# Conditioning of a two-layer diffusion block folded vector by vector: layer 1's residual and second-norm vectors for the latent stream only

## The reference, cut to what matters

```
sh1, sc1, g1, sh2, sc2, g2 = split(c_act  @ w_mod[l] + b_mod[l])     # latent stream
mod_c                      = split(cc_act @ w_mod[l] + b_mod[l])     # context stream
h  = rms_norm(x, ln1_g) * (1 + sc1) + sh1;   proj = h @ w_in[l]
x  = x + g1 * merge(three branches of proj) @ w_o
h2 = rms_norm(x, ln2_g) * (1 + sc2) + sh2
x  = x + g2 * (silu(h2 @ w_ff1) * (h2 @ w_ff3)) @ w_ff2
```

## Time and profile before

| | us |
|---|---|
| median of three runs | 1314.69 (1313.2 to 1316.62) |
| the profiled execution | 1312.58 |
| its span | 1310.8 |
| TensorE busy | 1233.6 (94% of the span) |
| VectorE busy | 915.6 (70%) |
| ScalarE busy | 531.1 (41%) |
| mean granted TensorE clock | 0.981 of full speed |

### The profile page before, as it was taken

One profiled execution on the slowest core, in us unless ns is written; L12 is line 12 of the kernel. 1 busy time (PEld: TensorE's weight loads), 2 busy tenths in 40 slices (PEclk: granted clock), 3 DMA queues, 4 the chain that ended last, 5 costly groups with the idle time before them and its releaser, 6 DMA issues.

```text
span 1310.8 us, 19521 instructions
## 1 busy us (share of the span) xinstructions
PE 1233.6 (94%) x7212; PEld 1031.6 (79%) x7212; DVE 915.6 (70%) x1372; ACT 531.1 (41%) x876; POOL 53.5 (4%) x52
## 2 busy tenths in 40 slices
PE   4999999999997979999999999779999998999997
PEld 3777766677876868887888788468888888999997
DVE  4554777768777777764676677777788876666565
ACT  4432555522423344322322223245664555544444
POOL 2000000000000300000000000200000002000002
PEclk9999999999998989999999999889999999999999
DMA  8837322024466516644565554324433574666562
GB/s 281 250 98 238 96 56 65 33 77 117 116 190 193 157 52 195 191 148 147 155 180 156 165 161 125 101 80 124 114 107 97 152 202 129 192 178 192 174 175 69
DMA packets 281599, 187.63 MB, mean 143 GB/s; under 512 B 12795, under 2 KB 270129, under 8 KB 281521
## 3 DMA queue, kind: packets, MB, share of 16 engines
q1 hardware_dynamic: 281521, 186.57, 48.6%
HBM read 185.49 MB, written 1.05 MB: 142 GB/s over the span
## 4 chain that ended last, share of the span: by engine, by line
PE 83%; DVE 8%; issue 4%; ACT 3%; DMA 1%; ACTq 0%; DVEq 0%; SPq 0%; POOL 0%; POOLq 0%
PE bank L1633 20%; PE bank L1635 20%; PE bank L1634 20%; PE scores L1885 2%; PE bank L1668 2%; PE bank L1669 2%; PE bank L1676 2%; DVE Wlo L355 2%; PE bank L1868 2%; PE probsT L1894 2%; PE bank L1870 2%; PE bank L1869 2%; ACT Whi L344 1%; PE attended L1905 1%; DVE RSTD L1149 1%
## 5 line engine op out<-in xcount | busy, mean ns | idle before, releaser
L1633 PE MATMUL bank<-Hhi,Whi 128*128 128x512 f32 (+2 forms) x1216 | 413.7, 340 | 6.4 <-DVE Wlo L355 6.4
L1635 PE MATMUL bank<-Hhi,Wlo 128*128 128x512 f32 (+2 forms) x1216 | 409.6, 337 | 0.0
L1634 PE MATMUL bank<-Hlo,Whi 128*128 128x512 f32 (+2 forms) x1216 | 409.6, 337 | 0.0
L355 DVE TENSOR_TENSOR Wlo<-Wraw,Whi 128x1024 fp32r<-128x1024 f32 (+4 forms) x328 | 320.5, 991 | 112.5 <-ACT Whi L344 110.9
L344 ACT ACTIVATE Whi<-Wraw 128x1024 fp32r<-128x1024 f32 (+4 forms) x330 | 277.6, 862 | 152.3 <-PE bank L1635 94.7
L1633 PEld LDWEIGHTS bank<-Hhi,Whi 128*128 128x128 f32 (+1 forms) x1216 | 229.9, 189 | 37.7 <-DVE Wlo L355 7.0
L1634 PEld LDWEIGHTS bank<-Hlo,Whi 128*128 128x128 f32 (+1 forms) x1216 | 230.0, 189 | 25.8 <-issue 1.2
L1635 PEld LDWEIGHTS bank<-Hhi,Wlo 128*128 128x128 f32 (+1 forms) x1216 | 229.9, 189 | 25.1
L1633 PE MATMUL bank<-Uhi,Whi 128*128 128x512 f32 (+1 forms) x480 | 164.3, 342 | 0.7 <-DVE Ulo L1161 0.6
L1634 PE MATMUL bank<-Ulo,Whi 128*128 128x512 f32 (+1 forms) x480 | 162.7, 339 | 0.0
L1635 PE MATMUL bank<-Uhi,Wlo 128*128 128x512 f32 (+1 forms) x480 | 162.5, 339 | 0.0
(11 more groups left out here) (169 smaller groups left out, 1412.2 us busy)
## 6 DMA issues: line engine op xcount, KB each, us to landing
Wraw<-in_w_ff SPq DMA_DIRECT2D x120, 512.0 KB, 3.8
Wraw<-in_w_in SPq DMA_DIRECT2D x78, 512.0 KB, 3.8
ATT<-in_w_mod SPq DMA_DIRECT2D x56, 512.0 KB, 4.2
Wraw<-in_w_o SPq DMA_DIRECT2D x16, 512.0 KB, 4.7
ACC<-in_w_mod SPq DMA_DIRECT2D x12, 512.0 KB, 3.9
Wraw<-in_w_ff SPq DMA_DIRECT2D x16, 384.0 KB, 3.2
Wraw<-in_w_mla_o SPq DMA_DIRECT2D x8, 512.0 KB, 3.4
PR<-in_w_mod SPq DMA_DIRECT2D x8, 512.0 KB, 4.3
```

What stands on the lines that cost most here:

```text
L355: last = eng.tensor_tensor(lo, raw, hi.bitcast(F32), ALU.subtract)
L1633: pe.matmul(dst, sh, mh, start=j == 0, stop=False)
L1634: pe.matmul(dst, sh, ml, start=False, stop=False)
L1635: last = pe.matmul(dst, sl, mh, start=False, stop=j == k - 1)
```

## The change

Folds now go by vector, not by turns of two. In the branches only vector 4 of layer 0 is folded (8 transfers, both streams). Along the FFN come seven vectors of 8 transfers: vector 5 of layer 0 (both streams), vectors 0 and 1 of layer 1 (both), vectors 2 to 5 of layer 1 (latent stream only: one fold instruction instead of two, and half the matmuls of the sum). The sums over 256 columns stand behind FFN tiles 14, 24, 34, 42, 50, 58 and 66; the transposes (two instead of four) one tile behind each, and those of the last at the start of layer 1. VectorE adds each vector to MOD in the tile of its transposes; vector 5 of layer 0 is read from tile 16 on. ScalarE's part of layer 0's FFN is written out instead of looped. In the projection the last four transfers of vectors 2 and 3 are issued later: 12 and 13 behind the load of chunk 14, 14 and 15 behind that of chunk 15, before behind chunks 12, 13, 14 and 15.

```diff
-HALF_AFTER_LOOK = [10, 11, 17, 18, 19, 21, 22, 23, 26, 27, 30, 31, 32, 33, 34, 35]
-TURN_AFTER_LOOK = [b + j for b in (0, 24) for j in (2, 4, 5, 6, 8, 9, 10, 12, 13, 14, 16, 17, 18, 19, 20, 21)]
-TURN_AFTER_LOOK += [48 + j for j in (0, 1, 2, 4, 5, 6, 7, 8, 9, 10, 12, 13, 14, 15, 16, 17)]
+BRANCH_FOLDS = [10, 11, 18, 19, 22, 23, 26, 27]
+FF_VECTORS = [(0, 5, 2), (1, 0, 2), (1, 1, 2), (1, 2, 1), (1, 3, 1), (1, 4, 1), (1, 5, 1)]
+FF_FOLDS = [4, 5, 6, 8, 9, 10, 12, 13, 14, *range(16, 27), 28, 29, 30, 32, *range(33, 65)]
+FF_SUMS = [14, 24, 34, 42, 50, 58, 66]
...
-                        for m in range(0, 4) if n == 7 else (2 * n - 12, 2 * n - 11) if n < 12 else (n,):
-                            mod(0, 1, m // 2, m % 2, "projection")
+                        ahead_of = {7: 4, 8: 6, 9: 8, 10: 10, 11: 12, 14: 14, 15: 16}
+                        while at.mod.n < ahead_of.get(n, 0):
+                            mod(0, 2 + at.mod.n % 2, at.mod.n // 2, "projection")
...
-            def fold(raw, k, acc, done):
-                for s in range(2):
+            def fold(raw, k, streams, acc, done):
+                for s in range(streams):
...
+            def fold_channels(c):
+                n, v, k = at.mod.n, c // STEPS, c % STEPS
                 dve.wait_ge(mod_in[n % MSLOTS], 16 * (n // MSLOTS + 1))
+                if k:
+                    dve.wait_ge(mod_used, n)
+                elif v > 1:
+                    dve.wait_ge(summed, v)
+                fold(mod_slot(n % MSLOTS, "channels"), k, FF_VECTORS[v][2], lambda s: ff_acc(v, s), mod_used)
                 at.mod.next()
...
+            def over_inputs(streams, acc):
+                n = T // 2
+                pe.wait_ge(mod_rows, at.turn)
+                for s in range(streams):
                     for j in range(4):
+                        last = pe.matmul(S[0][32 * j:32 * (j + 1), 0:n], ROWSEL[:, 31 - s:63 - s],
+                                         acc(s)[:, j * n:(j + 1) * n], start=s == 0, stop=s == streams - 1)
+                last.then_inc(summed, 1)
+            def sum_branch():
+                pe.wait_ge(branch_used, STEPS)
+                over_inputs(2, branch_acc)
+            def sum_channels(v):
+                pe.wait_ge(mod_used, TURN + STEPS * (v + 1))
+                over_inputs(FF_VECTORS[v][2], lambda s: ff_acc(v, s))
...
-                    half_done = l == 0 and HALF_AFTER_LOOK[STEPS - 1] // 4 == g - 1
-                    group(CO0, (lambda: sum_half(0)) if half_done else None)
+                    group(CO0, sum_branch if l == 0 and g == BRANCH_FOLDS[-1] // 4 + 1 else None)
...
+                    def tile_over():
+                        if l == 0 and seen in FF_SUMS:
+                            sum_channels(FF_SUMS.index(seen))
+                        if l == 0 and seen - 1 in FF_SUMS[:-1]:
+                            mod_turn(2)
+                        seen += 1
...
-                        down(7)
-                        sum_turn(g)
-                        down(1)
-                        if not last:
-                            mod_turn()
+                        down(8)
```

More of the change, by code:

```diff
@@ L264, in build @@
         mod_used = sem("mod_used")
-        half_in = [sem(f"half_in{b}") for b in range(2)]
-        half_used = sem("half_used")
-        turn_summed = sem("turn_summed")
+        branch_in = [sem(f"branch_in{b}") for b in range(2)]
+        branch_used = sem("branch_used")
+        summed = sem("summed")
         selector = sem("selector")
@@ L989, in _, with hidden @@
                 normed_h(l, 3, NS[l])
-                h0 = 0
+                seen = 0
+                def tile_over():
+                    nonlocal seen
+                    if l == 0 and seen in FF_SUMS:
+                        mod_row()
+                    seen += 1
                 for g, n in enumerate(FF_GROUPS):
                     last = g == len(FF_GROUPS) - 1
-                    with at.loop(act, n // 2, chunks=4, tiles=4, operands=2) as i:
+                    def hidden(i):
                         for j in range(2):
@@ L1007, in _ @@
                             at.operand.next()
+                            tile_over()
+                    if l == 0:
+                        for i in range(n // 2):
+                            at.ring = 0
+                            hidden(i)
+                        at.ring = 0
+                    else:
+                        with at.loop(act, n // 2, chunks=4, tiles=4, operands=2) as i:
+                            hidden(i)
                     if last:
@@ L1014, in _ @@
                             residual_squares(j)
-                    else:
[L1016 to L1025, removed]
+                    elif last:
+                        for j in range(8):
+                            look()
+                            residual_squares(j)
+                            tile_over()
+                        at.ring = 0
+                    elif l == 0:
+                        for j in range(8):
+                            look()
+                            at.tile()
+                            tile_over()
+                        at.ring = 0
+                    else:
+                        with at.loop(act, 2, chunks=4, tiles=4):
+                            for j in range(4):
                                 look()
                                 at.tile()
[L1028 to L1035, removed]
                 root(SEQ if l == DEPTH - 1 else T, D)
@@ L1712, in mod_step @@
                         last.then_inc(mod_used, 1)
-            def over_inputs(dst, src):
-                for s in range(2):
+            def over_inputs(streams, acc):
+                n = T // 2
+                pe.wait_ge(mod_rows, at.turn)
+                for s in range(streams):
                     for j in range(4):
[L1718 to L1732, removed]
+                        last = pe.matmul(S[0][32 * j:32 * (j + 1), 0:n], ROWSEL[:, 31 - s:63 - s],
[7 more added lines that the diff above has]
+                over_inputs(FF_VECTORS[v][2], lambda s: ff_acc(v, s))
             def first_steps(part):
```

108 lines of the change are left out of this document (55 added, 53 removed).

## The result

The changed kernel takes 1297.0 us (median of four runs, 1295.0 to 1299.3) against 1313.95 us before (median of four): ratio 0.9867, 95% interval 0.9851 to 0.9884, so 1.2 to 1.5% faster. Four more runs, made later, gave 0.9881 (0.9863 to 0.9899); the eight together have a median of 1298.4 us and lie in a lower and an upper part, 1295 to 1296 and 1298 to 1300; no single run lies at the 1297.0. Forecast were 1295.0 us, between 1289 and 1302. The profiled execution has a span of 1293.5 us, 17.3 less than before, where the sum said 19.7.

What follows compares the result with a forecast made beforehand. TensorE, busy 94% of 1310.8 us, was taken as the bound. Terms -1.8 - 6.5 - 1.4 + 1.8 + 0.5 - 12.0 - 0.3 gave -19.7 us: 1295.0 us, range 1289 to 1302, forecast's chance 0.60.

Steps and rivals of the forecast that it cites:

- Projection: Projection, gap before tile 13: later transfers let loads 13 and 14 pass, -1.8 us; bounds 0 and -1.8.
- Crossing: Branches into output projection: two fold pairs leave, 6.97 us gap becomes 2.2; with the clock -6.5 us, bounds -4.8 and -8.8.
- so I count this 1.8 us as won too: Crossing into the output projection: clock stays at 1.00 behind the remaining 2.2 us gap, saving 1.8 us.
- rival A: Clock still falls after the crossing's 2.2 us gap, or near the end: 1.8 us, up to 3; 1297 to 1298; chance 0.14.
- the forecast's own list of what would show it wrong: FFN sum or transpose waiting over 1 us, low clock at the crossing, or last-group down tiles over 4.1 us each.
- The row on which I leaned: Layer 1's crossing before the change: clock stayed 1.00 after gaps of 2.1 and 1.2 us.
- Sums and transposes: Branches: one sum fewer, -1.4 us; FFN: first six sums +1.8, their transposes +0.5, new waits 0.
- rival D: FFN: transposes wait for ScalarE's row copy, six times; at 10 us 27 us lost, 1322; chance 0.03.
- for the reason given: Branches' sum, moved to group 7: last fold stands at the same position, so its wait of about 1.3 us stays.
- The last sum: Last FFN down group: one fold less ends the wait before the sum, -12.0 us; bounds -8.3 and -12.4.
- Rival C: VectorE remains the bound at the last group; TensorE waits 1 to 4 us if slack is exceeded; 1296 to 1301; chance 0.08.
- The forecast's step from the rule: Last down group: GpSimd's addition delays VectorE wherever it falls, one fold less does not shorten that; period 4.08 us.

Runs made afterwards that it cites:

- the later sum: Changed kernel with the sum over the branches' vector behind the second gate tile of group 7 instead of the first: 1292.6 us, ratio 0.9838.
- the last sum with both streams: Changed kernel with layer 1's vectors 2 to 5 folded, summed and added for both streams again: 1304.4 us, ratio 0.9921.
- the reordered crossing: Changed kernel with ScalarE's high parts before its last branch look, VectorE's low parts among its last Z and G, its last look behind them: 1289.2 us.

## Why the prediction was right, and where it was off

The waits went and stayed where the forecast had them; two terms of the clock were mis-sized, and they make the whole difference of 2.4 us in the profile. In the medians, 2 to 3.5 us off, the low clock that some runs have in layer 1 comes on top.

**Projection.** Forecast -1.8, in place -1.9 in the profiles. What the forecast did not see is that this gain need not be kept: alone the edit made no difference in the time, and undone in the changed kernel none that four runs can tell.

**Crossing.** The gap of 6.97 us became 2.2, as worked out: 406.36 to 408.78 below, less the 0.23 of one product, against the earlier trace rows. But the step "so I count this 1.8 us as won too" failed. The clock fell behind 2.2 us as behind 7:

```profile
406.36 0.39 PE L1694 MATMUL bank<-Hhi,Wlo 128*128 128x512 f32 x1
408.78 1.09 PE L1701 MATMUL bank<-Hlo,Whi 128*128 128x512 f32 x2 [2.03 <-DVE Hlo L1174]
```

```profile
408.70:412.20 3.50, 3.42 (x8) 0.54 0.31 92
```

This was rival A, at 0.14, and low clock at the crossing was on the forecast's own list of what would show it wrong. The row on which I leaned, layer 1's crossing at 1.00 in one execution, was a single draw (and the row ends before the second of the two gaps, though the trace has 1.00 behind that too): in the changed kernel that crossing shows 1.00 in one profile and low clock in the next, and in the one profile with the old issue order the first crossing stays at 1.00.

**Sums and transposes.** A two-stream sum takes 1.32 us from product to product as forecast; the one-stream sum 702.37 to 703.25, 0.88, where 0.90 was worked out:

```profile
702.37 0.39 PE L1660 MATMUL bank<-Uhi,Wlo 128*128 128x512 f32 x1
702.69 0.64 PE L1745 MATMUL scores<-G,ROWSEL 128*32 128x256 f32 x8
703.25 0.50 PE L1658 MATMUL bank<-Uhi,Whi 128*128 128x512 f32 x1
```

At none of the thirteen sums and transposes in the FFN does TensorE wait, so rival D had nothing. The wait of the branches' sum stayed at 1.2 us, for the reason given: the later sum removes it.

**The last sum.** Forecast 5.1 us from the product before it to the total against 17.12; measured 826.55 to 831.65, 5.10:

```profile
826.55 0.39 PE L1660 MATMUL bank<-Uhi,Wlo 128*128 128x512 f32 x1
826.87 0.64 PE L1745 MATMUL scores<-G,ROWSEL 128*32 128x256 f32 x8
827.43 0.50 PE L1658 MATMUL bank<-Uhi,Whi 128*128 128x512 f32 x1
...
831.65 1.02 PE L1716 MATMUL bank<-SUM,ONES 128*128 128x512 f32 x2
```

VectorE in that group of the changed kernel:

```profile
806.73 0.87 DVE L1540 SCALAR_TENSOR_TENSOR X<-bank,MOD,X 128x256 f32<-128x256 f32 x2
...
808.65 2.32 DVE L1117 SCALAR_TENSOR_TENSOR G<-ATT,CV,G 128x1024 f32<-128x1024 f32 x1
810.89 0.86 DVE L1540 SCALAR_TENSOR_TENSOR X<-bank,MOD,X 128x256 f32<-128x256 f32 x2
...
812.81 1.27 DVE L1117 SCALAR_TENSOR_TENSOR G<-ATT,CV,G 128x1024 f32<-128x1024 f32 x1
```

GpSimd in the same stretch:

```profile
808.41 1.48 POOL L608 TENSOR_TENSOR SUM<-SUM,V 128x512 f32<-128x512 f32 x1 [2.68 <-ACT V L706]
812.93 2.31 POOL L608 TENSOR_TENSOR SUM<-SUM,V 128x512 f32<-128x512 f32 x1 [3.04 <-ACT V L706]
```

VectorE's period is 4.16 us (806.73 to 810.89), a little over TensorE's 4.08, where 4.08 was forecast. Its fold and GpSimd's addition overlap in each of the group's five tiles with a fold, and which of the two is long goes by which started first: where GpSimd's addition is ahead by 0.24 us (808.41), the fold takes 2.32 us and the addition 1.48; where the fold is ahead by 0.12 (812.81), the fold takes 1.27 and the addition 2.31. In that tile VectorE gave the lag back. Rival C was thus true in its condition, but the slack of two tiles swallowed it. By the port rule of the Trainium skill ("GPSIMD Engine Reference", section "Key points") VectorE's instructions with two SBUF inputs contend with GpSimd; the trace agrees, with 1.05 us for one fold. The forecast's step from the rule, that an addition costs VectorE its delay wherever it falls, does not hold in the tile of 812.81: there GpSimd paid it.

**Low clock behind the first total.** It held 5.3 us of products, at 0.50, where I had left the old 3.7, and that costs 0.8 us: this is the other mis-sized term, counted at 0.

```profile
461.50:466.80 5.30, 5.28 (x13) 0.50 0.00 0
```

Whether the length of a low stretch follows from the moment at which the gap falls, or from something else that an edit moves, these runs don't settle. They show only that it changes, between 2.8 and 5.3 us of products behind the same gap of 6.7 us and between 3.6 and 6.1 behind the crossing's of 7, and that keeping TensorE busy removes it.

## What to carry to other kernels

An engine that is busy two thirds of the time is the bound only at a few places; find them as waits of the engine that sets the pace, and ask of each fold or copy which instruction queued behind it somebody waits for. Ending side work two tiles before its consumer took 5.4 of the last wait's 7.9 us here, and doing less of it took the rest; by the estimate above the second alone would have taken most as well, so how the two share it depends on which comes first. On a TensorE-bound kernel count a gap like these, of 2.2 us or more, as the gap plus what the low clock may cost behind it, take neither the presence nor the absence of low clock from one profile, and try to fill such gaps, with moved work or even with matmuls that nobody reads.

## What the runs showed of the hardware that was not expected

The granted clock fell to 1.2 GHz behind gaps of 2.2 us in both profiles of the changed kernel's crossing (0.54 in the window behind the first) and stayed at 2.4 GHz behind the same gap with the old issue order (1.00), and behind the wait of 2.5 us before the last sum with both streams (1.00). A saving upstream of 1.9 us was worth nothing over ten runs. Of a fold on VectorE and an addition on GpSimd that overlap, the one that started second took the delay, in all five tiles of the changed kernel's last down group (2.31 to 2.32 us for the fold in four, 2.31 for the addition in one). Matmuls without use in the gaps, 15 in all, made the kernel 5 to 6.5 us faster with no other change, and with the reordered crossing too the clock is 1.00 over everything from 38 to 1273 us of a span of 1282.8:

```profile
38.00:1273.00 1235.00, 1211.45 (x7075) 1013.52 (x7067) 854.39 (x1303) 510.82 (x847) 46.66 (x40) 1.00 0.49 142
```
